# Routed experts on gathered token blocks, and 24 modulation tiles placed elsewhere, in a two-block transformer kernel

## What is computed

```python
def _hierarchical_moe(u, ...):                 # 256 tokens, 4 groups of 4 experts, hidden 256
    p_group = jax.nn.softmax(tf @ w_rg + b_rg)
    g_val, g_idx = lax.top_k(p_group, 1)       # every token goes to ONE group
    in_group = e_logits[g_idx]
    e_val, e_idx = lax.top_k(in_group, 2)      # and to two experts of that group
    weights = g_val[:, None] * jax.nn.softmax(e_val, axis=-1)
    ...
    for e in range(N_EXPERTS):
        hidden = jax.nn.silu(t @ w_gate[e]) * (t @ w_up[e])
        y = y + gate[:, e:e + 1] * (hidden @ w_down[e])

# second block, per layer (2 layers)
mod = silu(c) @ w_mod[l] + b_mod[l]            # 6144 values; the same for c_ctx
sh1, sc1, ga1, sh2, sc2, ga2 = jnp.split(mod, 6, axis=-1)
h = modulate(rmsnorm(x, g_norm1[l]), sh1, sc1)
... projections, mixer, attention ...
x = x + ga1 * (concat @ w_out[l])
x = x + ga2 * sqrelu_mlp(modulate(rmsnorm(x, g_norm2[l]), sh2, sc2), w_up[l], w_down[l])
```

## Time and profile before

| | |
|---|---|
| median of three runs | 1597.4 us |
| the profiled execution | 1598.57 us, span 1596.5 us |
| PE busy | 1538.2 us (96%), 9912 matmuls |
| DVE busy | 1068.6 us (67%) |
| ACT busy | 758.7 us (48%) |
| ring pieces loaded by SP | 350 of 512 KB, 4.2 us from issue to landing in the median |
| expert layer | from about 284 to 557 us of the span |
| projections of layer 0 | from about 575 to 683 us |

### The profile page before, as it was taken

The page is one execution under the profiler, slowest core; times in us unless marked ns, Lnnn a source line. Parts: engine busy times, 40 slices in busy tenths (PEclk is TensorE's granted clock), DMA queues, the critical chain, the costliest instruction groups (busy, mean ns, idle before and its releaser), DMA issues.

```text
span 1596.5 us, 27225 instructions
## 1 busy us (share of the span) xinstructions
PE 1538.2 (96%) x9912; PEld 1350.9 (85%) x9912; DVE 1068.6 (67%) x1834; ACT 758.7 (48%) x1302; POOL 99.4 (6%) x167
## 2 busy tenths in 40 slices
PE   8999999999999999998899999999999998999997
PEld 7998798999999978755687888888887885899997
DVE  5877496898888889325846554555567845765554
ACT  5544554544444563435635531254225355574562
POOL 0011000000000000000200000001000002000000
PEclk9999999999999999999999999999999999999999
DMA  9675173587778723312142644455452442246562
GB/s 342 238 258 188 47 229 98 209 261 257 256 257 255 231 75 106 103 43 52 29 145 98 214 163 157 142 192 193 145 157 86 130 109 40 88 152 187 180 184 92
DMA packets 71785, 254.91 MB, mean 160 GB/s; under 512 B 7920, under 2 KB 11152, under 8 KB 71456
## 3 DMA queue, kind: packets, MB, share of 16 engines
q1 hardware_dynamic: 54048, 189.43, 36.2%
q0 software_dynamic: 17664, 64.49, 13.5%
HBM read 252.78 MB, written 1.11 MB: 159 GB/s over the span
## 4 chain that ended last, share of the span: by engine, by line
PE 86%; DVE 8%; ACT 3%; issue 3%; DMA 0%; DVEq 0%; ACTq 0%; SPq 0%
PE pair L1101 85%; PE pair L1145 1%; DVE sq L2360 1%; ACT wh L601 1%; DVE uv L1789 1%; DVE sq L1829 1%; DVE small L1821 1%; PE pair L1290 0%; ACT sq L669 0%; DVE wl L1748 0%; ACT rstd L638 0%; DVE ul L1778 0%; DVE res L2513 0%; DMA res<-in_x 0%; ACT rstd L640 0%
## 5 line engine op out<-in xcount | busy, mean ns | idle before, releaser
L1748 DVE TENSOR_TENSOR wl<-ring,wh 128x1024 fp32r<-128x1024 f32 x350 | 426.6, 1223 | 201.7 <-ACT wh L601 197.5
L601 ACT ACTIVATE wh<-ring 128x1024 fp32r<-128x1024 f32 x350 | 366.7, 1052 | 249.8 <-PE pair L1101 233.7
L1101 PE MATMUL pair<-uh,wh 128*128 128x256 f32 (+3 forms) x1280 | 417.0, 326 | 8.0 <-DVE ul L1780 5.2
L1101 PE MATMUL pair<-uh,wl 128*128 128x256 f32 (+3 forms) x1280 | 412.7, 322 | 0.0
L1101 PE MATMUL pair<-ul,wh 128*128 128x256 f32 (+3 forms) x1280 | 411.5, 322 | 0.0
L1101 PEld LDWEIGHTS pair<-uh,wh 128*128 128x128 f32 (+1 forms) x1280 | 235.5, 184 | 34.2 <-issue 8.4
L1101 PEld LDWEIGHTS pair<-uh,wl 128*128 128x128 f32 (+1 forms) x1280 | 235.2, 184 | 24.0
L1101 PEld LDWEIGHTS pair<-ul,wh 128*128 128x128 f32 (+1 forms) x1280 | 235.3, 184 | 23.4
L1101 PE MATMUL pair<-hh,wh 128*128 128x512 f32 (+1 forms) x512 | 172.9, 338 | 1.2 <-DVE res L2513 1.2
L1101 PE MATMUL pair<-hh,wl 128*128 128x512 f32 (+1 forms) x512 | 171.7, 335 | 0.0
L1101 PE MATMUL pair<-hl,wh 128*128 128x512 f32 (+1 forms) x512 | 170.7, 333 | 0.0
(11 more groups left out here) (304 smaller groups left out, 2432.8 us busy)
## 6 DMA issues: line engine op xcount, KB each, us to landing
ring<-in_w_stream SPq DMA_DIRECT2D x350, 512.0 KB, 4.2
mod_w<-in_mods POOLq DMA_DIRECT2D x48, 512.0 KB, 3.8
uh_f<-in_mods POOLq DMA_DIRECT2D x42, 512.0 KB, 5.1
qk_w<-in_mods POOLq DMA_DIRECT2D x6, 512.0 KB, 7.1
uv<-c_rows POOLq DMA_DIRECT2D x4, 512.0 KB, 7.2
ml<-ml_dram POOLq DMA_DIRECT2D x4, 512.0 KB, 7.6
table<-in_table SPq DMA_DIRECT2D x1, 1849.5 KB, 12.1
res<-in_x SPq DMA_DIRECT2D x4, 256.0 KB, 4.0
```

What stands on the lines that cost most here:

```text
L601: act.activation(wh[:, s, :], ring[:, s, :], ACT.Copy).then_inc(S("w_hi"), 1)
L1101: ins = pe.matmul(*operands, **flags)
L1748: tt(wl[:, s, :], ring[:, s, :], wh[:, s, :].bitcast(F32), ALU.subtract).then_inc(S("w_lo"), 1)
```

## The change

The largest of the four groups is found at run time. Its four experts (8 units) still run over all 256 tokens as before. The tokens of the three smaller groups are gathered into a block of 128 columns each, and each of their 12 experts ("crowd") runs over its group's block alone, with the tokens as the stationary operand and 512 weight columns moving; the results are put back by one-hot products.

```diff
@@ the order of the pieces: the experts' pieces are chosen at run time
+MOE_ORDER = [(0, j) for j in range(GROUP_PIECES - 1)]
...
+    if _e < N_CROWD:
+        GU.append(S_MOE + len(MOE_ORDER))
+        MOE_ORDER += [(1 + _e // EG, 6 * (_e % EG) + _j) for _j in range(4)]
...
+        DN.append(S_MOE + len(MOE_ORDER))
+        MOE_ORDER += [(1 + (_e - 1) // EG, 6 * ((_e - 1) % EG) + 4 + _j) for _j in range(2)]
@@ SP
+            pieces(RING, S_MOE)
+            at_group = []
+            for t, (g, j) in enumerate(MOE_ORDER):
+                if g and len(at_group) == 1 or not at_group:
+                    sp.wait_ge(S("moe_first"), 1 + len(at_group))
...
+                        at_group.append(sp.value_load(first_i[0:1, k:k + 1], min_val=lo,
+                                                      max_val=lo + (NG - 1) * GROUP_PIECES))
+                n = S_MOE + t
+                piece(n % RING, w_stream[at_group[g] + j], n + 1 - RING)
@@ PE, ahead of the first unit
+            turn_tokens(0)
+            turn_tokens(1)
+            turn_logits()
+            turn_tokens(2)
+            turn_tokens(3)
+            pe.wait_ge(S("rt_group"), 1)
...
+            last.then_inc(S("rt_counted"), 1)
+            turn_over(MOE_SPIN, 5)
@@ PE, the crowd
+            pe.wait_ge(S("xg_lo"), KT)
+            crowd_gate_up(0, range(KT))
+            down(N_UNIT - 1)
+            for e in range(N_CROWD):
+                if e + 1 < N_CROWD:
+                    crowd_gate_up(e + 1, range(4))
+                crowd_turn(e)
+                if e + 1 < N_CROWD:
+                    crowd_gate_up(e + 1, range(4, KT))
+                crowd_down(e)
+            for g in (1, 2):
                 for o in range(KT):
...
+                    scatter(g, o)
@@ ACT, one expert of the crowd
+                split(GU[e] + 3 + AHEAD)
+                act.wait_ge(S("crowd_up"), e + 1)
+                act.activation(eg[:, e % 2, :], bank[4 + e % 2][:, 0:T], ACT.Silu,
+                               scale=slots[:, g - 1, 4:5]).then_inc(S("crowd_silu"), 1)
@@ DVE, ahead of the first unit
+            for c in range(4):
+                turned_rest(c)
+            add_squares("ctx", 512)
+            ts(hidl[:, 1, 0:P], ones, 0.0, None, ALU.mult).then_inc(S("moe_zero"), 1)
+            lo_end[0] = N_PIECES
+            split(S_MOE + 1)
@@ the modulation tiles of layer 0: 6 in the units, 16 in the projections, 8 in the MLP
+MOD_UNIT = (0, 1, 1, 1, 1, 1, 1, 0)
+MOD_IN = MOD_MOE + sum(MOD_UNIT)
+MOD_LATE = MOD_IN + 16
...
+                    if l == 0:
+                        mod_tiles(1, in_spent[:, :] if j < 11 else pair[3][:, :])
...
+                        if half == 0 and j % 2:
+                            late_gate(i, j // 2)
```

More of the change, by code:

```diff
@@ L811, in moe_unit @@
                 act.activation(hidh[:, a % 2, :], eg[:, a % 2, :], ACT.Copy).then_inc(S("moe_hi"), 1)
[L812 to L821, removed]
+                if a:
+                    split(S_MOE + 3 * a + 4)
@@ new lines, in down, with gather @@
+            def down(a):
+                pe.wait_ge(S("moe_lo"), a + 1)
+                parts(UNIT_DOWN[a])
+                for o in range(KT):
+                    prod(bank[(y0 + o // 2) % 4][:, (o % 2) * T:(o % 2 + 1) * T], UNIT_DOWN[a], o, hidh[:, a % 2, :],
+                         hidl[:, a % 2, :], False, False, skip_group_check=True)
+            def gather(f):
+                if f >= 2:
+                    pe.wait_ge(S("xg_lo"), f - 1)
+                o = bank[6 + f % 2][:, 0:3 * P]
+                for b in range(TB):
+                    for x in (uh, ul):
+                        last = mm(o, tok_major(x, b, f), pick[:, b, :], start=(b == 0 and x is uh),
+                                  stop=(b == TB - 1 and x is ul))
+                last.then_inc(S("xg_full"), 1)
@@ L1433, in _ @@
             last.then_inc(S("gate_full"), 1)
[L1434 to L1443, removed]
+            pe.wait_ge(S("moe_zero"), 1)
@@ L1459, in _ @@
[L1459 to L1467 removed]
+                       skip_group_check=True).then_inc(S("moe_cleared"), 1)
@@ new lines, in _ @@
+            gate_up(1)
+            pe.wait_ge(S("norm_rstd"), NORM["ctx"] + 1)
+            for b in range(TB):
+                mm(slot_of[:, b * P:(b + 1) * P], dest[:, b, :].to_broadcast([P, P]), ident, start=True, stop=True)
+            pe.wait_ge(S("pick_set"), 1)
+            for g in range(1, NG):
+                for b in range(TB):
+                    last = mm(slot_sums[:, 8 * g - 8:8 * g - 3], pick[:, b, crowd(g)].bitcast(F32), tok_v[:, b, 0:5],
+                              start=(b == 0), stop=(b == TB - 1))
@@ new lines, in _, with crowd_gate_up @@
+            last.then_inc(S("slots_full"), 1)
+            down(0)
+            for a in range(2, N_UNIT):
+                gate_up(a)
+                down(a - 1)
+                if a == 2:
+                    pe.wait_ge(S("slots_set"), 1)
+                if a < 6:
+                    gather(2 * a - 4)
+                    gather(2 * a - 3)
+            def crowd_gate_up(e, ks):
+                g = 1 + e // EG
+                for k in ks:
+                    if k % 2 == 0:
+                        parts(GU[e] + k // 2)
+                    last = prod_t(bank[4 + e % 2], GU[e] + k // 2, k % 2 * 512, 512, xgh[:, k, crowd(g)],
+                                  xgl[:, k, crowd(g)], k == 0, k == KT - 1)
+                if k == KT - 1:
+                    last.then_inc(S("crowd_up"), 1)
```

499 lines of the change are left out of this document (334 added, 165 removed).

## The result

The changed kernel takes **1586.2 us** in the median of four runs (1584.9 to 1588.7), against 1597.3 for the kernel before on the same chip: a ratio of 0.9925, 95% interval 0.9903 to 0.9947. So 11 us were won where 27 were forecast. The profiled execution has a span of 1583.1 us, 13.4 less than before.

What follows compares the result with a forecast made beforehand. PE was taken to bound the kernel (86% of the chain). Terms: -255.9 + 20.4 + 67.1 + 116 + 6.5 - 1 + 18.3 + 1 - 0.5 = -28.1, forecast 1570 us; range 1560 to 1581 (chance 0.5), 8 in 10 1550 to 1591.

Steps and rivals of the forecast that it cites:

- the ring's round: Crowd: four pieces share a round of landing plus 2.6 us; 18 rounds for 72 pieces, 116 us.
- L: Time for a weight piece to land after its load is issued; taken as 3.85 us in the crowd.
- the quiet row: Measured landings from 580 to 700 us, where pieces come one at a time: median 3.5 us.
- the signs to look for: Expected in the profile of after, among others: crowd 116 us, steps 9.7 us apart, landings 3.6 to 4.2 us.
- B: Rival: slow ring in the crowd, landings of 5.7 us, crowd 149 us, kernel 1603 us; chance 0.12.
- rival D: Routing and projections both at upper bounds, or mv's starved products at a lower clock: +14, 1584 us; chance 0.13.
- Rival A: Quick ring, landings of 3.0 to 3.4 us; PE sets the crowd's pace, 101 to 107 us, kernel 1557; chance 0.17.
- Routing: Ahead of the experts: the first unit's products wait for the routing and no longer hide it, +20.4 us.
- Units: Largest group's seven gate/up units and eight downs, with gather and small products: 67.1 us.
- Tail: End of the experts: last expert's uncovered transposes, high and low part 1.0 us, scatter 5.5; together 6.5 us.
- Projections: Layer 0's projections: 14 more modulation tiles of 2.4 us on a nearly full DVE, +18.3 us.
- The eight tiles of the MLP: Eight modulation tiles (19 us) on DVE, busy 57 of 100 us in the MLP: claimed hidden.

## Why the prediction was right and wrong

**Which mechanism.** Right. The forecast named the ring's round as what binds the crowd, and the chain, the waits and four experiments bear it out.

**The step that failed** is a term of the sum: L. "I take L = 3.85, between the first two and nearer the quiet one, as only the ring's own pieces meet." It was 4.8, which is 18 x 0.95 = 17 us; the twelve experts by their own spacing took 131.5 for 116. That is about the 16 us between the forecast 27 and the measured 11, but not because all else was right: units and tail missed by 6 us more, and the projections and the step behind the experts gave 7 us back. The reason given for L was the mistake: the ring's own pieces are enough to crowd each other. The median of 3.5 belongs to a stretch in which PE takes a piece every 5.6 us; in the crowd a load is issued every 1.86 us and takes 4.8, so 2.6 are under way at a time. With half the bytes L is 2.9, with eight slots 5.3. The nearest row was the one of the units before (4.5, at 258 GB/s), and with 4.5 the crowd comes out at 128 us. Leaning to the quiet row, whose stretch moved 101 GB/s, for one that I myself had put at 325 was not consistent. In the crowd itself landing and traffic rise together (4.7 us at 285 GB/s, 5.2 at 331, 5.3 at 375 with four, five and eight slots), so L and the pace have to be solved together. The GB/s alone don't give L, though: the stretch from 60 to 140 us moved 259 GB/s, as the units did, and had 5.7, with other queues beside the ring. No run here shows what makes that difference. Of the signs to look for, the landings of 3.6 to 4.2 us and the spacing of 9.7 did not come (4.8 and 10.96), ACT's wait for a DMA did. "Landings are over 5 us (B)" did not come either; 4.8 lies over half of the way from 3.85 to B's break-even of 5.4. The time itself lies beside rival D's 1584, by coincidence: neither the routing nor the projections reached D's upper bounds.

By the Trainium skill, in "DMA: Bandwidth & Descriptors", section "Anatomy of one DMA — SWDGE (gpsimd) path", a load costs a fixed 2.0 us and its bytes at 436 GB/s: an estimated 3.2 us for a piece and 2.6 for half a piece. The runs gave 4.8 and 2.9, on SP's queue and with two to three under way at a time. So the measured landings decide, and they are longer. Rival A, whose time the rule gives too, did not come about with four slots; with eight its crowd of 101 to 107 us did, but with landings of 5.3 us, for another reason.

**Routing.** Right: +20.3 for +20.4. DVE's small steps ran from 288.91 to 298.96, 10.05 us for 8.8 + 1.0; PE's first product came at 305.02, with 9.5 us of idle time ahead of it for 11; the clock cost 1.8 for 2.

**Units.** 66.5 us to the first crowd product, and 2.8 for the last down that is mixed into the crowd: 69.3 for 67.1.

**Tail.** 6.5 forecast, of which 5.5 for the scatter; it took 5.8. But ahead of it lie the last expert's uncovered steps and products at a falling clock:

```profile
519.58 0.50 PE L1207 MATMUL pair<-wh,hidh 128*128 128x512 f32 x1 [2.26 <-DVE hidl L2399]
522.67 0.63 PE L1207 MATMUL pair<-wh,hidh 128*128 128x512 f32 x1
522.00:524.00 2.00, 2.00 (x7) 1.52 (x6) 1.28 (x2) 1.06 (x1) 0.00 (x0) 0.50 0.86 303
```

PE idled 2.9 us in two pauses around the last transposes (1.0 forecast). Then the clock fell to 0.50, and the last twelve products took 4.4 us instead of 2.8. Together this is 4 us that the forecast did not have. The pauses within the crowd are not what brought the clock down. With half the bytes PE was full from 400 to 480 us, paused 3.1 us at this same place, and the clock fell as well:

```profile
498.00:500.00 2.00, 2.00 (x6) 1.52 (x6) 1.07 (x1) 0.90 (x1) 0.00 (x0) 0.50 0.88 340
```

With eight slots PE paused 1.6 us there, and the clock stayed at 1.00.

**Projections.** Mechanism right, size near: first to last `qkp`-to-`pf` emptying (549.8 to 669.4) is 119.6 us for 103.1 before (579.6 to 682.7), +16.5 for +18.3. DVE is busy for 58.8 of 60.2 us and PE waits for `wl` (9.1 us in 5 waits up to 640 us), as forecast. But the whole stretch to the first product on `lw` grew by only 13.7, since the 2.8 us behind `pf` came back: before, the clock was 0.50 at this place; after, it is 1.00:

```profile
672.00:674.00 2.00, 2.00 (x10) 1.26 (x10) 0.00 (x0) 0.26 (x2) 0.82 (x2) 1.00 0.00 0
```

Why it stays up there isn't settled.

**Small ones.** The eight tiles of the MLP are hidden, as forecast. The experts' end to the first `qkp` bank gave 3.2 for 1, and it recurs in every run (19.8 to 20.4 us for 23.3). PE idles 2.6 us of this stretch before, nearly all in waits for DVE's `ul`, and 0.4 after. So the mechanism is the forecast one, DVE's `ctx` work starting earlier, with 2.3 us for 1; the last 1 us was not looked for. The 2.2 us of the start can't be put down to `lw`: the same step, which nothing of the experiments touches, starts between 286.3 and 291.0 us in the other runs.

The sum again with what was measured: routing +20.3, experts -44.7, ctx -3.2, projections +13.7, and the start, the MLP and layer 1 with what their spread brings, +0.5: -13.4, the difference of the two spans.

## What to carry to other kernels

Where a change speeds up a stage that streams its weights, ask for the round of a buffer slot (issue, landing, conversion) divided by the number of slots before anything else, and take the landing from a stretch with the traffic that the faster stage will itself make, not from a quiet one, or give both and let the range span them. Such a bound shows as a stage in which no engine is full and a chain that goes DMA, converter, DMA; more slots then help even though each landing gets longer. The idle time of an engine that is a part of the round is not spare.

## What the hardware showed that I had not expected

- SP's queue brought 375 GB/s over 80 us with eight slots and 285 with four. Each landing took 5.3 us in the first case (5.6 in the second run with eight slots, at 371 GB/s) and 4.7 in the other: with more loads under way the throughput was a third higher and the wait an eighth to a fifth longer. The share of time that the DMA engines were busy, 0.87 with four slots, looked near its limit and was not; it reached 0.99 with eight.
- A piece of 256 KB landed in 2.9 us where one of 512 KB took 4.8, both with four slots: halving the bytes took off 40% of the time.
- PE idled 14% of the crowd in short pauses, and the granted clock stayed at 1.00 all through it. It fell to 0.50 only behind the pauses at its end (0.7 and 2.3 us), and it did so behind one of 3.1 us in a run without pauses before it.
